# A Fourier branch on 129 mirrored positions, an out-projection that starts with its SSM half, and a new order of its chunks

## What is computed

```
h      = modulate(rms_norm(x), shift, scale)            # 256 x 2048
proj   = h @ w_in
fr     = fftn(proj[:, :1024] as 4 groups of 256, axes=(tokens, channels of the group)).real
y_four = fr @ w_fmix[g]                                 # per group, 256 x 256
y_ssm  = group_rms_norm(ssd(proj) * silu(z))            # 256 x 1024
x      = x + gate * rms_norm(concat(y_four, y_ssm) @ w_out)
q, k   : top 16 experts for each of 8 heads and each token
x      = x + gate * rms_norm(sum_e gate_e * gelu(h2 . u_e) * v_e)
```

## Time and profile before

| | us |
|---|---|
| median of 3 runs | 1913.82 (1911.83 to 1916.88) |
| the profiled execution, own time | 1911.74 |
| its span in the profile | 1909.9 |
| Fourier stage on PE | 397 to 460 |
| out-projection on PE | 460.4 to 577.9 |
| first expert gather | 597.3 |

### The profile page before, as it was taken

How to read it: one execution, slowest core, us unless ns; L and a number is a source line. 1 busy time by engine, 2 the same in 40 slices (tenths; PEclk the granted TensorE clock), 3 DMA queues, 4 the chain that set the end, 5 groups by cost and what they waited for, 6 DMA issues and landing times.

```text
span 1909.9 us, 12872 instructions
## 1 busy us (share of the span) xinstructions
PE 1538.7 (81%) x4425; PEld 701.9 (37%) x4425; DVE 1065.9 (56%) x1493; ACT 333.1 (17%) x859; POOL 780.1 (41%) x666
## 2 busy tenths in 40 slices
PE   2999999998999777777777777777777777777776
PEld 0434464565448622323233323223232323232232
DVE  0219777674218866564655646552964655646445
ACT  2101211121113211212121111112221111111111
POOL 0002233211004576545454554542774545454541
PEclk8999999999999899999999999999999999999998
DMA  9979887886456899999999999999999999999997
GB/s 388 396 276 343 325 316 275 309 323 231 137 205 259 358 406 421 422 422 421 421 422 421 422 422 421 422 421 422 400 421 421 422 422 421 422 421 421 422 422 293
DMA packets 132591, 713.02 MB, mean 373 GB/s; under 512 B 14192, under 2 KB 16816, under 8 KB 61104
## 3 DMA queue, kind: packets, MB, share of 16 engines
q0 software_dynamic: 92160, 604.02, 77.5%
q1 hardware_dynamic: 40368, 108.19, 15.0%
HBM read 709.97 MB, written 2.20 MB: 373 GB/s over the span
## 4 chain that ended last, share of the span: by engine, by line
DMA 57%; PE 30%; DVE 7%; POOL 4%; issue 2%; ACT 1%; SPq 0%; DVEq 0%; POOLq 0%; ACTq 0%
DMA arena<-in_expert_v,arena 47%; PE PS L1266 7%; DMA arena<-in_expert_u,arena 6%; PE PS L1347 6%; PE PS L1559 5%; PE PS L1484 5%; POOL arena L489 4%; DMA arena<-in_w_mod 3%; DVE arena L1120 2%; PE PS L1225 2%; DMA arena<-in_w_in 1%; PE PS L1299 1%; PE PS L1361 1%; DVE arena L859 0%; PE PS L1211 0%
## 5 line engine op out<-in xcount | busy, mean ns | idle before, releaser
L1559 PE MATMUL PS<-arena 128*128 128x512 f32 x2016 | 943.1, 613 | 309.7 <-DMA arena<-in_expert_v,arena 309.7
L1120 DVE CUSTOM_DVE_ANT_0 arena<-arena 128x2048 f32<-128x2048 f32 x256 | 584.2, 2291 | 497.6 <-DMA arena<-in_expert_u,arena 496.9
L1559 PEld LDWEIGHTS PS<-arena 128*128 128x128 f32 x2016 | 369.1, 192 | 883.2 <-DMA arena<-in_expert_v,arena 506.1
L489 POOL DMA_INDIRECT arena<-in_expert_v,arena x256 | 368.3, 1439 | 448.4 <-PE PS L1559 413.8
L489 POOL DMA_INDIRECT arena<-in_expert_u,arena x256 | 315.6, 1233 | 261.5 <-DVE arena L1101 109.9
L774 ACT ACTIVATE arena<-arena 128x128 f32<-128x128 f32 x252 | 97.5, 400 | 774.6 <-PE PS L1559 773.2
L859 DVE SCALAR_TENSOR_TENSOR arena<-arena 128x1024 f32<-128x1024 f32 x120 | 161.7, 1348 | 27.0 <-DMA arena<-in_w_mod 24.0
L419 POOL DMA_DIRECT2D arena<-in_w_mod x128 | 68.3, 536 | 237.1 <-DVE arena L859 183.0
L1266 PE MATMUL PS<-arena 128*128 128x512 f32 (+1 forms) x384 | 155.3, 563 | 5.9 <-DMA arena<-in_w_in 4.3
L1484 PE MATMUL PS<-arena 128*128 128x512 f32 x256 | 113.7, 605 | 4.1 <-ACT arena L674 4.1
L1347 PE MATMUL PS<-arena 128*128 128x512 f32 x256 | 111.4, 593 | 0.0
(11 more groups left out here) (203 smaller groups left out, 776.5 us busy)
## 6 DMA issues: line engine op xcount, KB each, us to landing
arena<-in_w_mod POOLq DMA_DIRECT2D x128, 512.0 KB, 6.1
arena<-in_w_in SPq DMA_DIRECT2D x28, 1024.0 KB, 12.0
arena<-in_w_mod SPq DMA_DIRECT2D x16, 1024.0 KB, 17.0
arena<-in_w_mod SPq DMA_DIRECT2D x8, 2048.0 KB, 12.4
arena<-in_w_out SPq DMA_DIRECT2D x16, 1024.0 KB, 11.3
arena<-in_w_query SPq DMA_DIRECT2D x8, 1024.0 KB, 9.2
arena<-in_x SPq DMA_DIRECT2D x4, 1024.0 KB, 11.3
arena<-cum_rows SPq DMA_DIRECT2D x4, 1024.0 KB, 9.5
```

The costliest lines, as they stand in the source:

```text
L489: nc.gpsimd.indirect_dma_start(slot, None, table, bass.IndirectOffsetOnAxis(ap=idx[:, u % BUF, j:j + 1], axis=0),).then_inc(arrived, 16)
L1120: V.tensor_tensor_reduce(out=rows, in0=rows, in1=h2row[u // PH], scale=1.0, scalar=0.0, op0=ALU.mult, op1=ALU.add, accum_out=dots[:, u % B ...
L1559: ins = M(PS[:, 4 * blk + b, :], diag_slot[j % 8], vslot[m % NV][:, b * NQ:(b + 1) * NQ], start=first, stop=last)
```

## The change

1. `at_make` computes positions 0 to 128 only, 258 columns a matmul for 512; `yf_make` keeps the cosine product in bank 4 and the sine product in bank 5, 129 columns a matmul for 256, eight matmuls a group as before.
2. ACT's `yf_out` copies the sine product (128x258) to `odd`. DVE's new `yf_add` writes the sum to positions 0 to 128 of `catF` and the difference, in falling order, to 255 to 129. `yf_make(g)` waits for `yf_add(g-1)`.
3. On PE `at_make(3)` comes ahead of `pq(3)`, and `y_transposes(0)` ahead of `yf_make(3)`; unit (0,0) begins with its SSM half, transposes block 1, then does its Fourier half.
4. ACT's `y_squares(1)` comes ahead of the last group's copies, and its root stands apart.
5. The late tiles have five slots, and their quotas shift to after `yt_out(1)`; the two column sums move one unit or two later, the row transposition to (2,0).
6. The order becomes (2,0), (3,0), (2,1), (3,1) in the second half.

The diff, cut to its core:

```diff
+NF = 129
...
-LATE_QUOTA = [4, 1, 1, 9, 9, 8]
+LATE_QUOTA = [4, 1, 1, 4, 1, 21]
+LATE = 5
+OUT_ORDER = [(0, 0), (0, 1), (1, 0), (1, 1), (2, 0), (3, 0), (2, 1), (3, 1)]
...
-ROWS_AT = (1, 1)
-SUMS_AT = {(0, 0): 6, (1, 0): 7}
+ROWS_AT = (2, 0)
+SUMS_AT = {(1, 0): 6, (1, 1): 7}
...
-        AT = at(84, 1024).rearrange("p (b n) -> p b n", b=2)
+        AT = at(84, 4 * NF).rearrange("p (b m n) -> p b m n", b=2, m=2)
+        odd = at(86.5, 2 * NF).rearrange("p (b n) -> p b n", b=2)
...
-        tail_late = [at(136 + 4 * s, 1024) for s in range(TAILS)]
+        tail_late = [at(136 + 4 * s, 1024) for s in range(LATE)]
...
-                    sp.wait_ge(wo_ps, 2 * (i - R_OUT + 1))
+                    sp.wait_ge(wo_ps, OUT_ORDER.index((i - R_OUT, 1)) + 1)
...
-                pool.wait_ge(tail_used, 6 * KT if n < TAILS else 6 * KT + n - TAILS + 1)
-                tail_load(n % TAILS, 6 + n // KT, n % KT, tail_late)
+                pool.wait_ge(tail_used, 6 * KT if n < LATE else 6 * KT + n - LATE + 1)
+                tail_load(n % LATE, 6 + n // KT, n % KT, tail_late)
+            pool.wait_ge(tail_used, 8 * KT)
...
-                A(AT, PS[:, 2:4, :], ACT.Copy).then_inc(at_evac, 1)
+                A(AT, PS[:, 2:4, 0:2 * NF].rearrange("p b (m n) -> p b m n", m=2), ACT.Copy).then_inc(at_evac, 1)
...
             def yf_out(g):
                 act.wait_ge(yf_ps, g + 1)
-                A(catF[:, 2 * g:2 * g + 2, :], PS[:, 4, :].rearrange("p (b t) -> p b t", b=2), ACT.Copy).then_inc(yf_evac, 1)
+                A(odd, PS[:, 5, 0:2 * NF].rearrange("p (b n) -> p b n", b=2), ACT.Copy).then_inc(odd_evac, 1)
...
+            def y_root(c):
                 act.wait_ge(gvar_ready, c + 1)
                 A(grs[:, 2 * c:2 * c + 2], grs[:, 2 * c:2 * c + 2], ACT.Sqrt).then_inc(gstd_ready, 1)
             for g in range(GROUPS):
-                pq_out(g)
-                at_out(g)
                 if g == GROUPS - 1:
-                    y_squares(1)
+                    at_out(g)
+                    pq_out(g)
+                    y_root(1)
+                else:
+                    pq_out(g)
+                    at_out(g)
                 yf_out(g)
                 if g == 0:
                     y_squares(0)
+                    y_root(0)
+                if g == GROUPS - 2:
+                    y_squares(1)
...
             def wo_out(n, t):
-                act.wait_ge(wo_ps, 2 * n + t + 1)
+                act.wait_ge(wo_ps, OUT_ORDER.index((n, t)) + 1)
...
+                    if half >= 6:
+                        slot = (n - 6 * KT) % LATE
+                        times = 4 * KT // MORE_TAILS + (2 * KT // TAILS if slot < TAILS else 0) + (n - 6 * KT) // LATE + 1
...
+            def yf_add(g):
+                dve.wait_ge(odd_evac, g + 1)
+                even = PS[:, 4, 0:2 * NF].rearrange("p (b n) -> p b n", b=2)
+                step(tt(catF[:, 2 * g:2 * g + 2, 0:NF], even, odd, ALU.add))
+                tt(catF[:, 2 * g:2 * g + 2, 255:P:-1], even[:, :, 1:P], odd[:, :, 1:P], ALU.subtract).then_inc(yf_evac, 1)
             def y_gate(c):
                 dve.wait_ge(h_evac, 8)
                 tt(yssm[c], yssm[c], zrow[c], ALU.mult).then_inc(yg_ready, 1)
                 if c:
                     late_tiles(4)
+                    yf_add(2)
                 dve.wait_ge(gsq_ready, 2 * c + 2)
                 rs = grs[:, 2 * c:2 * c + 2]
...
+            yf_add(0)
...
             y_gate(0)
             late_tiles(2)
             o_add(2)
             o_add(3)
+            yf_add(1)
             late_tiles(3)
             y_add(1)
...
-                src = PS[:, 2 + 4 * c:4 + 4 * c, :].rearrange("p b (k t) -> p (b k) t", t=P)
+                src = PS[:, 6 - 4 * c:8 - 4 * c, :].rearrange("p b (k t) -> p (b k) t", t=P)
                 tt(catS[:, :, c * P:(c + 1) * P], src, nw, ALU.mult).then_inc(yt_evac, 1)
             yt_out(0)
+            yf_add(3)
             yt_out(1)
...
-                        ins = M(PS[:, 2 + b, :].rearrange("p (m n) -> p m n", m=2), frow[k][:, ch:ch + P], dft[:, k, 0:2, :],
-                                start=(k == 0), stop=(k == 1))
+                        ins = M(PS[:, 2 + b, 0:2 * NF].rearrange("p (m n) -> p m n", m=2), frow[k][:, ch:ch + P],
+                                dft[:, k, 0:2, 0:NF], start=(k == 0), stop=(k == 1))
...
-                for b in range(2):
-                    for n, (m, k) in enumerate(((0, 0), (0, 1), (1, 0), (1, 1))):
-                        ins = M(PS[:, 4, 256 * b:256 * b + 256], PQ[:, k, 256 * m + P * b:256 * m + P * b + P],
-                                AT[:, k, 256 * m:256 * m + 256], start=(n == 0), stop=(n == 3))
+                for m in range(2):
+                    for b in range(2):
+                        for k in range(2):
+                            ins = M(PS[:, 4 + m, NF * b:NF * b + NF], PQ[:, k, 256 * m + P * b:256 * m + P * b + P],
+                                    AT[:, k, m, :], start=(k == 0), stop=(k == 1))
...
-                pe.wait_ge(at_evac, 4) if c == 0 else pe.wait_ge(y_used, 2)
+                pe.wait_ge(at_evac, 4) if c else pe.wait_ge(y_used, 2)
                 for k in range(8):
-                    ins = nc.tensor.transpose(PS[:, 2 + 4 * c + k // 4, (k % 4) * P:(k % 4 + 1) * P],
+                    ins = nc.tensor.transpose(PS[:, 6 - 4 * c + k // 4, (k % 4) * P:(k % 4 + 1) * P],
                                               yssm[c][:, k * P:(k + 1) * P], ident)
...
             at_make(2)
             yf_make(2)
+            at_make(3)
             pq(3)
-            at_make(3)
+            y_transposes(0)
             yf_make(3)
-            y_transposes(0)
-            def w_out(n, t, k0, k1):
-                for k in range(k0, k1):
+            FOURIER, SSM = list(range(8)), list(range(8, KT))
+            def w_out(n, t, ks, start=True, stop=True):
+                for k in ks:
                     cat = catF if k < 8 else catS
                     ins = M(PS[:, (n % 2) * 2 + t, :], cat[:, k % 8, t * P:(t + 1) * P], wring[(R_OUT + n) % 2][:, k, :],
-                            start=(k == 0), stop=(k == KT - 1))
+                            start=(start and k == ks[0]), stop=(stop and k == ks[-1]))
                 return ins
-            pe.wait_ge(yf_evac, GROUPS)
-            for n in range(4):
-                ring_wait(R_OUT + n)
-                if n == 0:
+            for n, t in OUT_ORDER:
+                if t == 0:
+                    ring_wait(R_OUT + n)
+                if n >= 2:
+                    pe.wait_ge(wo_evac, OUT_ORDER.index((n - 2, t)) + 1)
+                if (n, t) == (0, 0):
                     pe.wait_ge(pq_evac, GROUPS)
-                    w_out(0, 0, 0, 8)
-                    w_out(0, 1, 0, 8)
+                    pe.wait_ge(yt_evac, 1)
+                    w_out(0, 0, SSM, stop=False)
                     y_transposes(1)
-                for t in range(2):
-                    if n == 0:
-                        pe.wait_ge(yt_evac, t + 1)
-                    if n >= 2:
-                        pe.wait_ge(wo_evac, 2 * (n - 2) + t + 1)
-                    ins = w_out(n, t, 0 if n else 8, KT)
-                    ins.then_inc(wo_ps, 1)
-                    if (n, t) == ROWS_AT:
-                        rows_transpose(2, 6)
-                    if (n, t) in SUMS_AT:
-                        column_sums(SUMS_AT[n, t], 4, 0)
+                    pe.wait_ge(yf_evac, GROUPS)
+                    ins = w_out(0, 0, FOURIER, start=False)
+                elif (n, t) == (0, 1):
+                    w_out(0, 1, FOURIER, stop=False)
+                    pe.wait_ge(yt_evac, 2)
+                    ins = w_out(0, 1, SSM, start=False)
+                else:
+                    ins = w_out(n, t, FOURIER + SSM)
+                ins.then_inc(wo_ps, 1)
+                if (n, t) == ROWS_AT:
+                    rows_transpose(2, 6)
...
-                    pe.wait_ge(h2T_evac, q + 1) if t else pe.wait_ge(wo_evac, 5 + q)
+                    pe.wait_ge(h2T_evac, q + 1) if t else pe.wait_ge(wo_evac, OUT_ORDER.index((2 + q // 2, q % 2)) + 1)
```

More of the change, by code:

```diff
@@ L251, in build @@
         o_ps, o_used = sem("o_ps"), sem("o_used")
-        pq_ps, pq_evac, at_ps, at_evac, yf_ps, yf_evac = sem("pq_ps"), sem("pq_evac"), sem("at_ps"), sem("at_evac"), sem("yf_ps"), sem("yf_evac")
+        pq_ps, pq_evac = sem("pq_ps"), sem("pq_evac")
+        at_ps, at_evac, yf_ps, odd_evac, yf_evac = [sem(n) for n in (
+            "at_ps", "at_evac", "yf_ps", "odd_evac", "yf_evac")]
         yg_ready, gsq_ready, gvar_ready, gstd_ready, yn_ready, yt_ps, yt_evac = [sem(n) for n in (
@@ L712, in _ @@
             act.wait_ge(tail_used, 8 * KT)
-            for n in range(4):
-                for t in range(2):
-                    wo_out(n, t)
-                    if (n, t) == ROWS_AT:
-                        rows_copy(6)
-                    if (n, t) == (3, 0):
-                        y_norm(0)
-                        x1_norm(0)
```

(24 more changed lines are left out.)

## The result

The changed kernel takes 1899.63 us (median of 5, 1895.51 to 1903.93) where the kernel before took 1913.82; the ratio is 0.9924 with a 95% interval of 0.9904 to 0.9943. It is 14.2 us faster; 1899 had been forecast. Its profiled execution took 1900.21 us with a span of 1898.4.

A forecast was written before the change was run, and what follows sets the result against it. Prediction: PE bounds nearly all from 397 us to the out-projection's end, broken by late tiles on DVE. 14.1 + 3.0 - 2.2 = 14.9 us off 1911.7 gives 1896.8, plus 2.1 makes 1899; range 1895 to 1902.

The forecast's parts named there:

- The Fourier matmuls: `at_make` and `yf_make`, four groups: shorter matmuls take 1.73 and 1.90 us a group, 13.0 us less PE work.
- rival (b): `yf_make`: weight loads bind the short matmuls at 0.19 us a record, giving 1902.5 us; chance 0.10.
- What is lost in group 1: Ahead of `y_state(3)`: DVE's `o_add(2)` starts only 0.9 us earlier, so PE stands idle 3.9 us.
- From there to the out-projection: From `y_state(3)` to the first out-projection matmul: PE, DVE and ACT walked through; it starts 14.1 us earlier.
- rival (c): Last Fourier groups: DVE and ACT hand-offs take 3 to 5 us longer than walked, giving 1903 us; chance 0.11.
- The out-projection: Same matmuls without the slow clock at their start: 114.5 us for 117.5, 3.0 us less; new unit order brings nothing.
- The clock: Behind the new idle ahead of `y_state(3)`: a clock fall is likelier than not, costing 1.6 to 3.0 us, taken as 2.2.
- rival (a): Ahead of `y_state(3)`: the clock stays up through the 3.9 us idle, 17.1 us less, giving 1896.7; chance 0.17.
- The sum: Whole kernel: 14.1 + 3.0 - 2.2 = 14.9 us less, 1896.8 profiled, 1899 as median.
- The cover: During the out-projection: the last late tiles end 8 to 14 us before `column_sums(7)` needs them at 504.
- Rival (e): Late tiles ahead of `column_sums(7)` come 5.7 us apart, ending 50 us behind it, giving 1949 us; chance 0.04.
- The ring load of chunk 3: SyncE's reload behind unit (1,1): takes 12.7 us of the 15.4 available, fitting by 2.7.

The follow-up runs named there:

- The filled idle: Changed kernel with four extra 512-column matmuls of constants on PE between `at_make(1)` and `y_state(3)`; 1902.29 us, ratio 0.9938.
- three slots: Changed kernel with three slots for the late tiles instead of five; 1903.72 us, ratio 0.9952.
- two slots: Changed kernel with two slots for the late tiles instead of five; 1929.04 us, ratio 1.0079.
- The repeat: Changed kernel run again unaltered, on the same chip as three of the other follow-up runs; 1898.79 us, ratio 0.9919.
- the tiles undone: Changed kernel with four slots and the old placing of late tiles, column sums and row transposition; 1918.82 us, ratio 1.0023.
- tiles alone: Kernel before with only the new five slots and placing of late tiles, column sums and row transposition; 1908.0 us, ratio 0.9970.
- the head was undone alone: Changed kernel with both first units' Fourier halves first and `y_transposes(0)` behind `yf_make(3)`; 1899.64 us, ratio 0.9926.

## Why the prediction was right, step by step

**The Fourier matmuls**: forecast 1.73 and 1.90 us a group, measured 1.74 and 1.84. That weight loads of 192 ns would bind the short ones, rival (b), did not happen.

**What is lost in group 1**: the two new operations of DVE were priced at 0.43 each, with bounds up to 1.7 for the pair; they take 0.43 and 0.42, so the write in falling order costs no more than the other, and the prediction's second estimate for the pair, 0.69, was too low. The idle ahead of `y_state(3)`: 3.9 forecast, 3.87 measured, released by `o_add(2)`.

**From there to the out-projection**: S to O was forecast as 446.3 - 397.0 = 49.3 without a fall of the clock. The filled idle measures 49.0; the changed kernel's 50.7 has the fall in it. PE's short waits, 0.69 ahead of `yf_make(2)` and 0.36 ahead of the first `w_out`, are there as walked through (0.9 and 0.6), so rival (c), longer hand-offs, did not come.

**The out-projection**: 114.5 forecast, 114.7 measured, at full clock from its first record. E to G did not change; the 0.66 us were hidden, as undoing the order shows from both sides.

**The clock**: a fall was taken as likelier than not and priced at 2.2 us. It came in all six profiles that have the idle of 3.87 us ahead of `y_state(3)`. From that start to the `pq` behind `yf_make(1)` these take 5.0 to 5.3 us in five and 6.2 with three slots, where the filled idle takes 3.57, so a fall costs 1.4 to 1.7 us, and 2.6 once. The Trainium skill's TensorE: Matmul & The Clock Gate, section HAM oscillation, warns of idle that re-throttles the array. The pair of runs with the idle and with the idle filled bears that out here, 3.59 us against 1.95 for the same four records. But the run with two slots has an idle of 3.56 us in the same place with no fall, and one of 3.49 ahead of `y_state(1)` with a fall, so the length of the idle alone does not settle it. On this term the forecast was right as a chance is right: rival (a), no fall, was near.

**The sum**: 14.9 us were forecast for the stretch, 15.5 measured in it; most of the difference is the clock's 1.7 for 2.2. The profiled execution nevertheless came at 1900.2 for a forecast of 1896.8, since S was 3.9 us late. For the same reason the first record and the end of the out-projection, at 451.7 and 566.3, missed the marks that had been named for them (446 to 449, 561 to 563); less the 3.9 both lie within them. I had taken S as fixed. That step was missing, and it could have gone either way. The median was forecast by adding the 2.1 us by which the profiled execution had lain under it; after the change the profiled execution lay 0.6 above it. That the median hit 1899 to 0.7 us is in part luck. The repeat, whose median is 15.0 us under that of the kernel before on its chip, is the better witness of the 14.9.

**The cover**: the tiles ended at 494.84 + 1.28 = 496.1, 44.5 us behind O, with 57.8 available; forecast was 44 to 50. Rival (e), the late tiles that come late, is real: two slots cross the point, and with tiles 3.6 us apart, where I had named 3.5 for the turn into a loss, the kernel is 15 us slower than before. The turn had been put too late for this kernel: with two slots 19 tiles wait for their loads and not 16, and I had priced neither the clock behind the wait nor the hold-up of `o_add(0)`. The ring load of chunk 3 had less room than I gave it. I had counted 12.7 us for the load and 2.7 to spare; it took 14.0 here and 14.4 in the run with the tiles undone, so 1.6 us were to spare here and 0.6 were missing there. That part of the walk was mis-sized, and only the column sum between made it harmless. Tiles and load did not meet: the last tile ended 13 us ahead of the load's release.

What the parts are worth cannot be added up: tiles alone give 7.1 us of S to E, all the rest without the tiles costs 2.7, both together give 15.5. Of that rest the head was undone alone (2.7 us) and the unit order (nothing); the short matmuls were never run by themselves, so their share is known only together with the new hand-offs.

## What to carry to other kernels

Ask of an engine's saved work which queue stands next behind it: here 13 us less on PE gave nothing, even a loss, until the other engine's queue had been cleared, and where it was not cleared (`o_add(2)`) the rest came out as idle and slow clock. Walk both queues instruction by instruction with durations from the trace; in this kernel that was good to a microsecond over 165, of which the clock's share could have been anything from nothing to 2.6. Time a load from its release to its landing, not from its first to its last full stretch of traffic. When totals scatter more than the effect, cut the profile at fixed moments and compare the stretches.

## What had not been expected of the hardware

The same code in front of S took 397.0 to 406.5 us over eleven profiled executions, with the mean granted clock between 0.99 and 0.95 from 100 to 395 us. The longest slow stretch stood in the state-space part at 345 us in both kernels that had S past 406, where 64 records of 64 columns took 12.85 and 12.96 us, with the granted clock at 0.50 from 346 us on; in the changed kernel they took 7.20, although PE was busy in all three. Why the clock fell there in some executions and not in others, none of these runs tells.
